# Odd-layer input projection: latents ahead of the last convolution slot, 512 and 320 columns wide, with ScalarE copies

## The chip, the cores and the metric

The kernel runs on one core of a Trainium2 chip. The metric is the device time of one execution in microseconds, the median of three runs. A profiled execution gives the trace; its rows are in microseconds from the start of its span.

## What is computed

Two layers of a diffusion backbone, batch 1, on 512 latent and 256 context tokens of width 1024, all in float32. The even layer is gMLP gating beside grouped-query attention; the odd layer, which is changed here, is a Conformer convolution beside multi-head latent attention. Each layer is followed by a gated ConvFFN. The odd mixer, cut to what matters:

```python
z = h_lat @ w_in                     # 1024 x (1024 conv, 512 zq, 256 zkv + 64 key rope)
c_lat = conformer_conv(z[..., :1024], conv_w, conv_b, ...)    # width 31, then channel norm, SiLU
q = mla_q(z[..., 1024:1536], g_cq, w_uq, cos, sin)            # rmsnorm, 512 -> 8 x (128 + 64), rope
k, v = mla_kv(z[..., 1536:], g_ckv, w_ukv, cos, sin)          # rmsnorm of 256, rope of 64, -> 8 x (128 + 128)
att = block_attention(q, [k_ctx, k], [v_ctx, v], scale)
o_lat = jnp.concatenate([c_lat, att], axis=-1) @ w_out
```

## The kernel before

Every weight matrix is cut into **slots** of 128 x 2048 floats (1 MB). SyncE loads slot n into one of two buffers (`w_load`); ScalarE rounds it (`round_hi`, L285) once slot n-2 is used; VectorE takes the rest (`take_lo`, L291); a product is then three matmuls, high x high, high x low, low x high. The semaphore `w_used` counts slots that TensorE has finished. VectorE and ScalarE carry out their instructions strictly in the order written, so the order in the code below is the plan.

The odd layer's projection is eight slots (`N_ODZ`). Slots 0 to 3 are convolution features: `feature_slot` puts 256 features with the weights stationary and 512 tokens moving, 48 matmuls of 512 columns. Between them VectorE forms G = a * sigmoid(b), and `conv_steps` spends single taps of the width-31 depthwise convolution (124 in all) wherever VectorE has room: `(0, 0, 8, 8, 12, 16, 12, 8)` in the slots, 16 in the query stage, 7 beside the keys and values, the other 37 two at a time beside the attention units. Slots 4 and 5 are the 512 features of zq, 256 each (`token_slot`, L335 to L337: tokens stationary, 256 columns moving, 4 token tiles); slots 6 and 7 are the 320 features of zkv with the key's rope part, 160 each, 6 token tiles. VectorE copies zq and zkv out of PSUM.

After slot 7 the **chains** run: ScalarE squares (L1476, L1482), VectorE the mean, GpSimd the power -1/2, VectorE the normalised value (L1979, L2032), TensorE transposes (L1668, L1681), VectorE `scaled` (gain, L2020), ScalarE rounds it (cqh, ckh), VectorE `low` (L2026). `UQ0` (L1692 to L1694, 4 token tiles, 48 matmuls) gives the rope part of the queries, copied by VectorE to QR, rotated (`rotate`), doubled by GpSimd to QRD. UQ0+1 and UQ0+2 give eight heads of queries into four PSUM banks, each copied by VectorE to QTn (L2064). `rope_transposes(0)` stands after head 5, `rope_transposes(4)` after head 7; the latter waits bank by bank for VectorE's `rope_lo` (L2070). Then follow keys and values (UKV0), and 32 attention units (8 heads x 4 query tiles).

The channel norm of the convolution (`CLN = 22`) is spread over the units: sum at unit 22, squares at 24 and 25, sum of squares at 28 (L1797), mean square and reciprocal at 29 (L2122, L2124), Sqrt on ScalarE at 30; the output projection `out_pe` waits for it, and for the modulation gate's row (L617, from `diag`).

## Time and profile before

| | |
|---|---|
| median of 3 runs | 1880.16 us (1879.54 to 1880.5) |
| profiled execution | 1880.5 us, span 1878.7 us |
| PE / DVE / ACT / POOL busy | 95% / 61% / 36% / 10% |
| mean granted TensorE clock | 0.977 of 2.4 GHz |
| odd layer's slots 2 to 7 | 1091.8 to 1168.9 us |
| from there to UQ0 | 15.0 us |
| attention units | about 1260 to 1406 us |

PE is TensorE's matmuls, PEld its weight loads, DVE VectorE, ACT ScalarE, POOL GpSimd. A displayed duration of a matmul is longer than its distance to the next one, because they are pipelined; what a stream costs is read from starts or from stretches. PEclk is the granted clock as a share of 2.4 GHz; 0.50 is 1.2 GHz.

### The profile page before, as it was taken

What the parts mean: (1) busy time and instruction counts of PE and PEld (TensorE: products, weight loads), DVE (VectorE), ACT (ScalarE), POOL (GpSimd) and SP (SyncE); (2) the same over time, 40 slices, a digit from 0 to 9 for tenths busy, and PEclk for the clock granted to TensorE, in tenths of its full rate; (3) what the DMA queues carried; (4) which work ended last, traced back from release to release, by engine and by line L of the source; (5) the groups of instructions that cost most, each with busy time, mean ns of one, the idle gap of its engine ahead of it and who ended that gap; (6) DMA issues with size and microseconds to landing.
All of it is one profiled execution on the core that took longest, in us unless ns stands there. A gap on an engine that the chain in (4) does not pass through costs nothing.

```text
span 1878.7 us, 24143 instructions
## 1 busy us (share of the span) xinstructions
PE 1779.5 (95%) x9514; PEld 1499.1 (80%) x9514; DVE 1140.5 (61%) x1714; ACT 671.4 (36%) x1095; POOL 179.4 (10%) x199
## 2 busy tenths in 40 slices
PE   6999799899999999999999999789988899999998
PEld 4777699777888888887777889569986788888776
DVE  4675567667666765644354778877855544344454
ACT  4342256534422122123343431144445432232342
POOL 1176400001200000000000200111210100000000
PEclk9999899999999999999999999899999899999999
DMA  8433000131234435522121121100002122322321
GB/s 352 155 112 113 23 1 2 57 101 46 101 117 153 146 137 189 193 72 84 45 90 47 56 103 68 45 23 1 2 10 103 68 90 91 110 89 89 112 91 67
DMA packets 30996, 166.80 MB, mean 89 GB/s; under 512 B 4144, under 2 KB 4656, under 8 KB 16688
## 3 DMA queue, kind: packets, MB, share of 16 engines
q1 hardware_dynamic: 29024, 163.60, 24.1%
q10 hardware_dynamic: 1872, 1.82, 0.3%
q8 instruction: 69, 1.13, 0.3%
q14 instruction: 31, 0.25, 0.0%
HBM read 163.31 MB, written 2.10 MB: 88 GB/s over the span
## 4 chain that ended last, share of the span: by engine, by line
PE 84%; DVE 6%; issue 4%; ACT 3%; POOL 1%; DVEq 1%; DMA 1%; POOLq 0%; ACTq 0%; SPq 0%
PE PS L302 12%; PE PS L304 12%; PE PS L306 12%; PE PS L603 8%; PE PS L605 7%; PE PS L604 7%; PE PS L1078 5%; PE PS L344 2%; PE PS L1066 2%; PE PS L345 2%; PE PS L346 2%; DVE w_lo L291 1%; PE PS L336 1%; PE PS L337 1%; PE PS L335 1%
## 5 line engine op out<-in xcount | busy, mean ns | idle before, releaser
L302 PE MATMUL PS<-HT,w_hi 128*128 128x512 f32 (+1 forms) x1232 | 377.7, 355 | 10.4 <-DVE HT L517 5.0
L304 PE MATMUL PS<-HT,w_hi 128*128 128x512 f32 (+1 forms) x1232 | 371.1, 350 | 0.0
L306 PE MATMUL PS<-HT,w_lo 128*128 128x512 f32 (+1 forms) x1232 | 370.1, 349 | 0.0
L291 DVE TENSOR_TENSOR w_lo<-w_raw,w_hi 128x2048 fp32r<-128x2048 f32 x103 | 237.1, 2303 | 157.8 <-ACT w_hi L285 153.6
L603 PE MATMUL PS<-w_hi,a_ring 128*128 128x512 f32 x680 | 277.1, 408 | 15.2 <-DVE a_ring L676 8.1
L604 PE MATMUL PS<-w_lo,a_ring 128*128 128x512 f32 x680 | 268.2, 394 | 0.0
L285 ACT ACTIVATE w_hi<-w_raw 128x2048 fp32r<-128x2048 f32 x103 | 196.3, 1906 | 157.5 <-PEq L635 69.4
L302 PEld LDWEIGHTS PS<-HT,w_hi 128*128 128x128 f32 x1232 | 206.4, 189 | 51.7 <-issue 6.5
L306 PEld LDWEIGHTS PS<-HT,w_lo 128*128 128x128 f32 x1232 | 207.2, 189 | 31.7
L304 PEld LDWEIGHTS PS<-HT,w_hi 128*128 128x128 f32 x1232 | 207.1, 189 | 30.4
L975 DVE SCALAR_TENSOR_TENSOR yb<-PS,cws,yb 128x511 f32<-128x511 f32 (+1 forms) x132 | 83.2, 658 | 169.2 <-ACTq L941 165.7
L603 PEld LDWEIGHTS PS<-w_hi,a_ring 128*128 128x128 f32 x680 | 129.7, 191 | 57.0 <-issue 27.3
L431 DVE SCALAR_TENSOR_TENSOR m_acc<-m_raw,sT,m_acc 128x1024 f32<-128x1024 f32 x112 | 145.6, 1331 | 27.8 <-DMA m_raw<-modu 22.9
L937 ACT ACTIVATE yb<-PS,cws 128x512 f32<-128x512 f32 x44 | 34.3, 780 | 347.2 <-PE PS L306 347.2
L604 PEld LDWEIGHTS PS<-w_lo,a_ring 128*128 128x128 f32 x680 | 129.8, 191 | 29.4 <-issue 3.4
L605 PE MATMUL PS<-w_hi,a_ring 128*128 128x512 f32 x340 | 135.4, 398 | 0.0
L826 POOL TENSOR_TENSOR rstd<-rstd,halfneg 128x1 f32<-128x1 f32 x20 | 12.6, 628 | 1223.2 <-DVE rstd L775 1223.2
L1964 DVE SCALAR_TENSOR_TENSOR cat_od<-G,ccw,cat_od 128x512 f32<-128x512 f32 x120 | 85.6, 756 | 3.0
L1131 DVE TENSOR_REDUCE rmax<-PS 128x1 f32<-128x768 f32 (+1 forms) x72 | 66.6, 925 | 32.1 <-PE PS L1041 23.2
L344 PE MATMUL PS<-w_hi,HT 128*128 128x512 f32 x192 | 77.3, 403 | 4.9 <-DVE HT L1847 4.0
L605 PEld LDWEIGHTS PS<-w_hi,a_ring 128*128 128x128 f32 x340 | 65.8, 194 | 14.5
L345 PE MATMUL PS<-w_lo,HT 128*128 128x512 f32 x192 | 76.0, 396 | 0.0
(309 smaller groups left out, 2811.9 us busy)
## 6 DMA issues: line engine op xcount, KB each, us to landing
w_raw<-wpack SPq DMA_DIRECT2D x103, 1024.0 KB, 4.8
m_raw<-modu SPq DMA_DIRECT2D x80, 512.0 KB, 4.2
mod_raw<-modw SPq DMA_DIRECT2D x8, 1024.0 KB, 12.2
X<-x SPq DMA_DIRECT2D x1, 2048.0 KB, 8.7
out<-X SPq DMA_DIRECT2D x4, 512.0 KB, 2.6
X<-ctx SPq DMA_DIRECT2D x1, 1024.0 KB, 10.9
alnb<-aln ACTq DMA_DIRECT2D x1, 512.0 KB, 4.3
csn<-rope_ev ACTq DMA_DIRECT2D x1, 256.0 KB, 2.6
```

The source lines that it names most:

```text
L285: nc.scalar.activation(w_hi[r][:, :], w_raw[r][:, :], ACT.Copy).then_inc(wh_ready, 1)
L291: nc.vector.tensor_tensor(w_lo[r][:, :], w_raw[r][:, :], w_hi[r][:, :].bitcast(F32), ALU.subtract).then_inc(wl_ready, 1)
L302: nc.tensor.matmul(o, wh, xh, start=start, stop=False)
L304: nc.tensor.matmul(o, wh, xl, start=False, stop=False)
L306: last = nc.tensor.matmul(o, wl, xh, start=False, stop=stop)
L344: nc.tensor.matmul(o, xh, w_hi[r][:, wc], start=k == 0, stop=False)
L345: nc.tensor.matmul(o, xh, w_lo[r][:, wc], start=False, stop=False)
L431: ops.scalar_tensor_tensor(out=acc[g][:, :], in0=raw[:, :], scalar=sT[:, k, g:g + 1], in1=acc[g][:, :], op0=ALU.mult, op1=ALU.add)
L603: nc.tensor.matmul(o, ah, w_hi[n % 2][:, wc], start=k == 0, stop=False)
L604: nc.tensor.matmul(o, ah, w_lo[n % 2][:, wc], start=False, stop=False)
L605: return nc.tensor.matmul(o, al, w_hi[n % 2][:, wc], start=False, stop=k == kt - 1)
L1078: last = nc.tensor.matmul(PS[:, 7, 0:w * P], V[:, k0 + j, c:c + P], PT[u % 2][:, j * w * P:(j + 1) * w * P], start=j == 0, stop=j == nk - 1)
```

## The change

The slots' order becomes conv 0, 1, 2, then zq (3, 4), zkv (5, 6), then conv 3 as slot 7. A latent slot now holds half of the 1024 input features (four k-tiles) for all its columns: zq with 512 columns, zkv with 320 (`wide` with a bank and a width), accumulating over two slots in PSUM. ScalarE squares and copies each finished tile; the zq chain goes to slots 5 and 6, the zkv chain to slot 7, the zq transposes into slot 6, those of zkv into UQ0. ScalarE also copies QR and the eight heads. The taps are spread anew (47 in the slots, 28 in the query stage); the channel norm is two units later, and its Sqrt is in the output projection. At the start of the kernel, `mod_products` waits for both halves of a chunk at once. QR moves to the start of region R_A. Most deleted lines are left out of the diff; they are in the listing above.

```diff
-        QR = at("QR", R_MOD, [P, LT, 512])
+        QR = at("QR", R_A, [P, LT, 512])
...
-        mod_landed = [sem(f"mod_landed{i}") for i in range(KD)]
+        mod_landed = [sem(f"mod_landed{i}") for i in range(4)]
...
+        def wide(n, t, k, bank=None, w=512):
+            r, o, wc = n % 2, PS[:, t if bank is None else bank, 0:w], slice(k % 4 * w, k % 4 * w + w)
...
+            pe.wait_ge(mod_landed[c], 32)
             for i in range(2):
-                pe.wait_ge(mod_landed[2 * c + i], 16)
...
-        CLN = 22
+        CLN = 24
+        CONV_SLOTS, CONV_BANKS = (0, 1, 2, 7), (0, 3, 0, 6)
+        ZQ_BANKS, ZKV_BANKS, CQ_BANKS = (3, 4, 2, 5), (6, 7, 0, 1, 3, 4), (2, 5)
...
+            def cq_hi(k):
+                act.wait_ge(S("odn", "aff"), k + 1)
+                dst = cqh[:, k, :] if k < 4 else ckh[:, k - 4, :]
+                nc.scalar.activation(dst, ev_t[k % 2][:, 0:LAT if k < 4 else TOK], ACT.Copy).then_inc(S("odn", "hi"), 1)
             for s in range(N_ODZ):
                 if s:
                     round_hi(act, OD0 + s + 1)
-                if s < 4:
+                if s in CONV_SLOTS:
...
                     act.wait_ge(w_used, OD0 + s + 1)
...
+                if s == 4:
+                    for t in range(LT):
+                        act.wait_ge(S("odz", "acc"), t + 1)
+                        nc.scalar.activation(zjunk[:, :], PS[:, ZQ_BANKS[t], :], ACT.Square, accum_out=ssq[:, t:t + 1])
+                        act.drain()
+                        nc.scalar.activation(zq[:, t, :], PS[:, ZQ_BANKS[t], :], ACT.Copy).then_inc(S("odz", "copy"), 1)
+                    act.drain().then_inc(S("odq", "ssq"), 1)
                 if s == 6:
...
+                    for t in range(NT):
+                        act.wait_ge(S("odz", "acc"), LT + t + 1)
+                        nc.scalar.activation(zjunk[:, 0:256], PS[:, ZKV_BANKS[t], 0:256], ACT.Square,
+                                             accum_out=ssq[:, 16 + t:17 + t])
+                        act.drain()
+                        nc.scalar.activation(zkv[:, t, :], PS[:, ZKV_BANKS[t], 0:320], ACT.Copy)\
+                            .then_inc(S("odz", "copy"), 1)
+                        if t < 4:
+                            cq_hi(t)
+                    act.drain().then_inc(S("odkv", "ssq"), 1)
+            round_hi(act, UQ0 + 1)
+            def rope_out(t):
+                act.wait_ge(S("odu", "rmm"), t + 1)
+                nc.scalar.activation(QR[:, t, :], PS[:, t, :], ACT.Copy).then_inc(S("odu", "qr"), 1)
+            rope_out(0)
+            rope_out(1)
+            cq_hi(4)
+            rope_out(2)
+            rope_out(3)
+            cq_hi(5)
+            def query_out(h):
+                act.wait_ge(S("odu", "qmm"), h + 1)
+                nc.scalar.activation(QTn[:, h, :], PS[:, h % 4, :], ACT.Copy).then_inc(S("odu", "q"), 1)
+            query_out(0)
             round_hi(act, UQ0 + 2)
+            for h in range(1, 6):
+                query_out(h)
             act.wait_ge(S("odn", "krt"), 1)
             for p in range(HEADS):
                 h = (p + 4) % HEADS
                 if p == 4:
+                    query_out(6)
+                    query_out(7)
...
-                if u == CLN + 8:
-                    act.wait_ge(S("cln", "var"), 1)
+            attn_act(act, "od", True, units(True), 192 ** -0.5, beside_units)
+            def beside_out(q):
+                if q == 2:
+                    act.wait_ge(S("cln", "var"), 2)
...
+            def zq_transposes(k):
+                pe.wait_ge(S("odq", "xn"), 1)
+                if k >= 2:
+                    pe.wait_ge(S("odn", "aff"), k - 1)
+                for t in range(LT):
+                    last = nc.tensor.transpose(PS[:, CQ_BANKS[k % 2], t * P:(t + 1) * P], zq[:, t, k * P:(k + 1) * P],
+                                               ident[:, :])
+                last.then_inc(S("odn", "tr"), 1)
             for s in range(N_ODZ):
                 n = OD0 + s
...
-                if s >= 2:
-                    pe.wait_ge(S("odz", "evac"), s - 1)
...
-                elif s < 4:
...
+                elif s in CONV_SLOTS:
+                    if s == 2:
+                        pe.wait_ge(S("odz", "evac"), 1)
+                    else:
+                        pe.wait_ge(S("odz", "copy"), LT + 2)
+                    last = feature_slot(s, n, LAT, bank=CONV_BANKS[CONV_SLOTS.index(s)])
+                elif s < 5:
+                    if s == 3:
+                        pe.wait_ge(S("odz", "evac"), 2)
+                    for t in range(LT):
+                        for k in range(4 * (s - 3), 4 * (s - 3) + 4):
+                            last = wide(n, t, k, ZQ_BANKS[t])
+                        if s == 4:
+                            last.then_inc(S("odz", "acc"), 1)
                 else:
-                    if s == 6:
+                    if s == 5:
...
+                        pe.wait_ge(S("odz", "evac"), 3)
+                    for t in range(NT):
+                        if s == 5 and t >= 4:
+                            pe.wait_ge(S("odz", "copy"), t - 3)
+                        for k in range(4 * (s - 5), 4 * (s - 5) + 4):
+                            last = wide(n, t, k, ZKV_BANKS[t], 320)
+                        if s == 6:
+                            last.then_inc(S("odz", "acc"), 1)
+                            if t < 4:
+                                zq_transposes(t)
+                if s in (4, 6):
+                    pe.drain().then_inc(w_used, 1)
+                else:
+                    last.then_inc(w_used, 1)
             def key_transposes(k):
                 if k == 4:
-                    pe.wait_ge(S("odn", "aff"), 2)
+                    pe.wait_ge(S("odkv", "xn"), 1)
+                    pe.wait_ge(S("odn", "aff"), 4)
                 elif k == 5:
-                    pe.wait_ge(S("odn", "aff"), 4)
+                    pe.wait_ge(S("odz", "evac"), 4)
                 else:
                     pe.wait_ge(S("odn", "aff"), 5)
                 for t in range(NT):
                     src = zkv[:, t, (k - 4) * P:(k - 3) * P] if k < 6 else kr2[:, t, :]
                     last = nc.tensor.transpose(ps2(4 + 2 * (k % 2), TOK)[:, t * P:(t + 1) * P], src, ident[:, :])
                 last.then_inc(S("odn", "tr"), 1)
...
+            pe.wait_ge(S("odz", "copy"), LT + NT)
             pe.wait_ge(S("odn", "lo"), 4)
             n = UQ0
...
                 last.then_inc(S("odu", "rmm"), 1)
+                if t in (1, 3):
+                    key_transposes(4 + t // 2)
...
+            TAPS = (0, 0, 10, 12, 13, 9, 3, 0, 24)
...
-                conv_steps((0, 0, 8, 8, 12, 16, 12, 8)[s], range(min(s, 4)))
-                if s == 7:
+                conv_steps(TAPS[s], range(min(s, 3)))
+                if s == 5:
                     dve.wait_ge(S("odq", "ssq"), 1)
...
                         .then_inc(S("odq", "mean"), 1)
...
                     for t in range(LT):
                         last = nc.vector.tensor_scalar(zq[:, t, :], zq[:, t, :], rstd[:, t:t + 1], None, ALU.mult)
                     last.then_inc(S("odq", "xn"), 1)
-                b = 3 * (s % 2)
-                dve.wait_ge(w_used, OD0 + s + 1)
+                if s == 6:
+                    scaled(0)
+                    scaled(1)
+                    low(0)
+                    scaled(2)
+                    low(1)
+                    scaled(3)
+                    low(2)
+                    low(3)
+                if s == 7:
...
+                    dve.wait_ge(S("odkv", "ssq"), 1)
...
+                        .then_inc(S("odkv", "mean"), 1)
+                    for t in range(LT):
...
+                    dve.wait_ge(S("odkv", "rstd"), 1)
+                    for t in range(NT):
+                        last = nc.vector.tensor_scalar(zkv[:, t, 0:256], zkv[:, t, 0:256], rstd[:, 16 + t:17 + t], None,
+                                                       ALU.mult)
+                    last.then_inc(S("odkv", "xn"), 1)
...
+            take_lo(dve, UQ0 + 1)
+            scaled(4)
+            conv_steps(2)
+            low(4)
+            scaled(5)
+            conv_steps(2)
+            low(5)
...
+                dve.wait_ge(S("odu", "qr"), t + 1)
...
+                rotate(dve, zz[:, :, :, 0], zz[:, :, :, 1], csd[:, 0, t, :].unsqueeze(1).to_broadcast([P, 8, 32]),
...
+                dve.drain().then_inc(S("odu", "rope"), 1)
+                if t == 1:
                     dve.wait_ge(S("odn", "tr"), 7)
                     nc.vector.tensor_copy(KRT[:, :], ps2(4, TOK)).then_inc(S("odn", "krt"), 1)
...
+                if t == 2:
+                    take_lo(dve, UQ0 + 2)
+            conv_steps(TAPS[8])
...
-                    nc.vector.tensor_scalar(mu[:, :], PS[:, 6, :], 1.0 / 512, EPS, ALU.mult, ALU.add)
+                    nc.vector.tensor_scalar(mu[:, :], PS[:, 6, :], 1.0 / 512, EPS, ALU.mult, ALU.add)\
+                        .then_inc(S("cln", "var"), 1)
...
+    conv = _slots_in(od, [np.concatenate([r(P * j, P * j + P), r(512 + P * j, 512 + P * j + P)]) for j in range(4)])
+    zq = [_k_cols(od[512 * h:512 * h + 512], r(1024, 1536)) for h in range(2)]
+    zkv = [_k_cols(od[512 * h:512 * h + 512], r(1536, 1856)) for h in range(2)]
+    slots += conv[:3] + zq + zkv + conv[3:]
```

## Rows read from the trace of the kernel before

**Rows 1.** Page: the span, then busy time and share of each engine
```profile
span 1878.7 us, 24143 instructions
...
PE 1779.5 (95%) x9514; PEld 1499.1 (80%) x9514; DVE 1140.5 (61%) x1714; ACT 671.4 (36%) x1095; POOL 179.4 (10%) x199
```

**Rows 2.** Busy time by stretch: length, PE, PEld, DVE, ACT, POOL, PEclk, DMA share, GB/s
```profile
1102.90:1113.70 10.80, 10.80 (x50) 8.93 (x49) 8.44 (x10) 2.40 (x2) 0.00 (x0) 1.00 0.29 97
1113.70:1136.70 23.00, 23.00 (x193) 23.00 (x192) 20.49 (x26) 4.32 (x3) 0.00 (x0) 1.00 0.27 93
1136.70:1168.90 32.20, 32.20 (x290) 32.13 (x288) 27.41 (x40) 6.51 (x10) 1.02 (x1) 1.00 0.19 66
1168.90:1183.90 15.00, 6.67 (x29) 5.56 (x28) 13.14 (x45) 6.85 (x17) 1.33 (x1) 0.66 0.00 1
1183.90:1196.90 13.00, 12.72 (x48) 10.08 (x49) 9.97 (x12) 1.88 (x4) 0.00 (x0) 0.87 0.23 81
1196.90:1234.20 37.30, 29.23 (x134) 23.33 (x134) 31.26 (x53) 9.94 (x11) 4.17 (x4) 0.91 0.08 29
```

**Rows 3.** Timeline of TensorE before UQ0: start us, us, instruction, [idle before, releaser]
```profile
1170.37 3.52 PE L1668 MATMUL PS<-ident,zq 128*128 128x128 f32 x16 [1.38 <-DVE zkv L1998]
...
1183.94 0.79 PE L1692 MATMUL PS<-w_hi,cqh 128*128 128x512 f32 x1 [0.71 <-DVE cql L2026]
...
1184.96 0.63 PE L1694 MATMUL PS<-w_hi,cql 128*128 128x512 f32 x1
1185.39 0.63 PE L1692 MATMUL PS<-w_hi,cqh 128*128 128x512 f32 x1
```

**Rows 4.** Timeline of TensorE, query stage
```profile
1213.61 0.80 PE L302 MATMUL PS<-cqh,w_hi 128*128 128x512 f32 x1 [4.83 <-DVE w_lo L291]
...
1221.23 1.91 PE L1706 MATMUL PS<-ident,QRD 128*128 128x128 f32 x16
...
1230.19 2.39 PE L1706 MATMUL PS<-ident,QRD 128*128 128x128 f32 x16 [1.60 <-DVE QS L2070]
1234.29 0.59 PE L302 MATMUL PS<-ckh,w_hi 128*128 128x512 f32 x2 [1.71 <-issue]
```

**Rows 5.** Timeline of ScalarE, first square of zq
```profile
1143.21 0.63 ACT L1476 ACTIVATE sg<-zq 128x512 f32<-128x512 f32 x1 [4.32 <-DVE zq L1993]
```

**Rows 6.** Timeline of VectorE, projection and query stage
```profile
1130.63 11.34 DVE L1964 SCALAR_TENSOR_TENSOR cat_od<-G,ccw,cat_od 128x512 f32<-128x512 f32 x16
...
1164.08 1.67 DVE L1979 TENSOR_SCALAR zq<-zq,rstd 128x512 f32<-128x512 f32 x4 [1.13 <-POOL rstd L484]
...
1199.96 0.69 DVE L2064 COPY QTn<-PS 128x512 f32<-128x512 f32 x1 [0.22 <-PE PS L306]
...
1203.21 0.69 DVE L2064 COPY QTn<-PS 128x512 f32<-128x512 f32 x1 [0.17 <-issue]
...
1229.35 2.52 DVE L2070 TENSOR_TENSOR QS<-PS,QS 64x512 fp32r<-64x512 f32 x4
1231.90 4.49 DVE L291 TENSOR_TENSOR w_lo<-w_raw,w_hi 128x2048 fp32r<-128x2048 f32 x2
```

**Rows 7.** Timelines of VectorE, TensorE and ScalarE, end of the attention
```profile
1397.16 3.35 DVE L2124 RECIPROCAL rs_b<-mu 128x512 f32<-128x512 f32 x1
...
1401.29 0.87 PE L1066 MATMUL PS<-ident,Pod 128*128 128x128 f32 x6 [1.79 <-DVE Pod L1142]
1403.07 2.93 PE L1078 MATMUL PS<-PTo,Vod 128*128 128x128 f32 x12 [0.90 <-ACT PTo L1117]
...
1416.16 2.08 PE L617 MATMUL PS<-diag,ones 128*128 128x512 f32 x2 [3.15 <-DVE diag L769]
...
1411.08 1.91 ACT L285 ACTIVATE w_hi<-w_raw 128x2048 fp32r<-128x2048 f32 x1 [8.07 <-DMA w_raw<-wpack]
```

**Rows 8.** Line 388 (mod_products): durations min/median/max, starts; then idle by releaser
```profile
L388 PE MATMUL PS<-mod_raw,s x64: 592/592/617, 20.7 to 55.5; 128*32 128x512 f32 x64
...
  issue: 3.3, 11
```

More of the change, by code:

```diff
@@ L323, in feature_slot @@
             return last
-        def token_slot(ns, n, tiles, width, between=lambda step: None):
-            b, r = 3 * (ns % 2), n % 2
-            last = None
-            for t in range(tiles):
-                o = PS[:, b + t // 2, (t % 2) * 256:(t % 2) * 256 + width]
-                for k in range(KD):
-                    between(t * KD + k)
-                    wc = slice(k * 256, k * 256 + width)
-                    xh, xl = (HT[:, t // 2, w, k, t % 2 * P:t % 2 * P + P] for w in range(2))
-                    nc.tensor.matmul(o, xh, w_hi[r][:, wc], start=k == 0, stop=False)
-                    nc.tensor.matmul(o, xh, w_lo[r][:, wc], start=False, stop=False)
-                    last = nc.tensor.matmul(o, xl, w_hi[r][:, wc], start=False, stop=k == KD - 1)
-            return last
-        def wide(n, t, k):
-            r, o, wc = n % 2, PS[:, t, :], slice(k % 4 * 512, k % 4 * 512 + 512)
+        def wide(n, t, k, bank=None, w=512):
+            r, o, wc = n % 2, PS[:, t if bank is None else bank, 0:w], slice(k % 4 * w, k % 4 * w + w)
             xh, xl = (HT[:, t // 2, w, k, t % 2 * P:t % 2 * P + P] for w in range(2))
@@ L2002, in _ @@
-            const_ready(dve, "csd", 1)
-            dve.drain()
-            for t in range(LT):
-                kr = zkv[:, t, 256:320].rearrange("p (i two) -> p i two", two=2)
-                rotate(dve, kr[:, :, 0], kr[:, :, 1], csd[:, 0, t, :], csd[:, 1, t, :], rA[:, 0:32], rB[:, 0:32])
-            for half in range(2):
-                nc.vector.tensor_copy(kr2[:, :, 64 * half:64 * half + 64], zkv[:, :, 256:320])
-            dve.wait_ge(S("odkv", "ssq"), 1)
-            nc.vector.tensor_scalar(rstd[:, 16:16 + NT], ssq[:, 16:16 + NT], 1.0 / 256, EPS, ALU.mult, ALU.add)\
-                .then_inc(S("odkv", "mean"), 1)
@@ L2176, in _k_cols @@
     kt = w.shape[0] // P
-    return w[:, cols].reshape(kt, P, len(cols)).transpose(1, 0, 2).reshape(P, SLOT)
+    out = np.zeros((P, SLOT), w.dtype)
+    out[:, :kt * len(cols)] = w[:, cols].reshape(kt, P, len(cols)).transpose(1, 0, 2).reshape(P, kt * len(cols))
+    return out
 def _rope(d_rot):
```

143 lines of the change are left out of this document (41 added, 102 removed).

## The prediction

> **What bounds the kernel now.** I read the page's busy shares first: TensorE is busy 95% of a span of 1878.7 us [rows 1], so time can come only from cheaper TensorE work or from the few gaps. The odd layer's input projection was then cut into stretches [rows 2]. In the first three of them PE is busy to the last tenth at a granted clock of 1.00: one convolution slot of 48 matmuls, 512 wide, takes 10.8 us (0.225 each); the two zq slots, 192 matmuls 256 wide, take 23.0 us (0.120 each); the two zkv slots, 288 matmuls 160 wide, take 32.2 us (0.112 each). Each token tile takes 8 k-tiles x 3 products per slot (4 tiles for zq, 6 for zkv; the (x) of a stretch counts a matmul that lies across its edge too). The reader should see that 160 columns cost almost as much as 256: the narrow ones pay for something other than columns, and the weight load beside them is busy 32.13 of 32.20 us.
>
> The fourth stretch is a gap: 15.0 us with 28 transposes in it. PE waits there for the copy of zkv, later for the scaled and low parts, and starts the query projection only at 1183.94 [rows 3], because the chain square, mean, power, normalise, transpose, scale, round, low runs with nothing beside it. The clock falls to its lower level (1.2 of 2.4 GHz: mean 0.66 in the gap) and is still 0.87 in the next stretch. The query stretch (1196.9 to 1234.2) is 37.3 us for about 29 us of PE work; it waits 4.83 us for VectorE's low part of slot UQ0+2, 1.60 for the rope's low parts, and 1.71 before the first key, which the row calls issue but which ends with the low part of UKV0 [rows 4, 6].
>
> **Part by part.** (a) zkv wide. 144 matmuls of 320 columns replace 288 of 160. No row has 320 columns; the nearest are 256 (0.120) and 512 (0.225), so the bounds are 17.3 and 32.4 us. On the line between them 320 lies at 0.147: 21.2 us, a gain of 11.0. I take this, since 256 is much nearer. The trace's 0.112 at 160 columns is what makes the gain. The Trainium skill, "TensorE: Matmul & The Clock Gate", section "Back-to-back issue gap", gives N/2.4 + 2.5 ns for an isolated pair, 69 ns at 160 columns and 136 at 320, by which the two forms would cost the same 19.8 us and this part would give nothing; the row of 112 ns contradicts it for this stream.
>
> (b) zq wide: 192 x 0.120 = 23.0 becomes 96 x 0.225 = 21.6, a gain of 1.4.
>
> (c) The gap. Its 15.0 us go. Put back: the 28 transposes, now inside slot 6 and UQ0, at 1.91/16 = 0.12 each [rows 4], 3.4 us; two TensorE drains after slots 4 and 6, at the 0.5 that UQ0's stretch leaves (13.0 less 48 x 0.225 and less the slow start of (d)), 1.0; and a new wait. In slot 6 the first zq transposes follow tile 0, and need zq normalised. After slot 4: ScalarE finishes the last square (0.63) and a copy of the same 512 columns (taken as 0.63, with 0.3 for the sum's read-out), then rounds slot 6's weights (1.9); VectorE takes the low part (2.2), 9 taps at 11.34/16 = 0.70 (6.3), the mean (0.2), waits for the power (1.1), normalises (1.7) [rows 5, 6, 7]. That is 14.8 and a wake-up or two, say 15.1. PE has slot 5 (10.6), tile 0 of slot 6 (1.8) and a drain (0.5): 12.9. So it waits about 2.2, and I charge 1.7 for a clock dip behind it: after the 1.38 us before the first transposes the clock fell [rows 2, 3], and eight matmuls at the lower level cost 1.7 below. Sum of (c): -15.0 + 3.4 + 1.0 + 2.2 + 1.7 = -6.7. Bounds of the wait and dip: 0 and 8.
>
> (d) UQ0 took 13.0 us; it starts at full clock when conv slot 7 runs straight before it. Gain 1.7: at 1183.94 PE began slow, one matmul every 0.43 [rows 3], and the 13.0 us hold room for about eight such, 8 x 0.2. Everything the wait ahead of UQ0 needs should be ready: the zq low parts end in slot 6, the last zkv copies soon after it, and slot 7's 10.8 us cover the zkv mean, the key's rope, and the normalising. UQ0's own cover is its weights, rounded a slot earlier.
>
> (e) Query stage. VectorE loses twelve copies (QR and QTn) of 0.69 [rows 6] to ScalarE, which is idle there, but gets 28 taps (2 + 2 + 24) where it had 16, and its rotations no longer alternate with heads. From UQ0's end its chain is: scale and low of k = 5 (1.0 each), 2 taps 1.4, four rotations at 3.25 (one head copy's start to the next) - 0.6 = 2.6 (10.4), KRT copy 1.0, low part of UQ0+2 2.2, 24 taps 16.9, four rope lows 2.5, low of UKV0 2.2: 38.6 until the first key. Before it was 37.3 from the same point. With the wake-ups I take +1.5. PE would finish its share (two slots of 10.8, 38 transposes 4.6, drains 1.0) in about 27 and so idles some 9 us: about 2 before UQ0+2's weights, about 7 before the last rope transposes. Bounds: -3 (VectorE gets ahead) and +9 (ScalarE's in-order queue, where `cq_hi(5)` stands before `query_out(0)` and the weight rounding before `query_out(1)`, holds banks or the rotations). The later scores hang on the same POOL chain as before: 0.
>
> (f) Attention. Taps left beside the units go from 37 to 42; they lie in units paced by PE, price 0, with 5 x 0.70 = 3.5 if no cover. The channel norm moves two units later. Its reciprocal takes 3.35 us on VectorE and stood before the normalising of the last unit: PE waited 1.79 for Pod and ran the last twelve value products in 2.93, slow [rows 7]. Now mean-square and reciprocal follow the last unit, and the Sqrt goes into the output projection. Gain 1.8 plus at most 1.4 of clock: I take 3.0, bounds 0 and 4. What replaces it: PE waits for `var` to reach 1, a copy and one 0.7 us read, then runs 24 products; but it stands 3.15 us at line 617 anyway, behind the DMA that starts at attention's end (ScalarE waits 8.07 for it) and VectorE's diag [rows 7]. If that cover is gone it costs 1.1. The Sqrt and its table load delay ScalarE's third part by some 1.9, under the same wait.
>
> (g) `mod_products` waits for both halves. Of its 64 matmuls none sat behind a DMA; the only idle before them is issue [rows 8]: the second half had landed. 0. The memory placements of QR and zjunk, the weight slots (eight still, 1 MB each) and SP's queue order: same count, same triggers, 0.
>
> **Sum:** -11.0 - 1.4 - 6.7 - 1.7 + 1.5 - 3.0 = -22.3. The profiled execution took 1880.5 us (1.8 beyond its span), 0.34 above the median of 1880.16; so 1858.2 for it, 1857.9 for the median.
>
> **Rivals.** *The query stage gives back more.* For it: it is already VectorE-bound, and 24 taps in one block stand before the rope lows that PE waits for. Against: the copies leave. At the bound of (e), 7.5 more: 1865. *No wait in slot 6.* If slot 5's taps end early, 3.9 more gained: 1854. *Width pays nothing:* at the upper bound of (a) 320 columns cost as 512 (0.225 each, 32.4 us), and (a) turns to zero: 1869. The section of the Trainium skill named in (a) would have it zero too. Against it: 256 columns cost 0.120. *The wait re-forms before UQ0:* PE needs the zq lows and all zkv copies there, and slot 7 as well as slot 5 wait for banks; if ScalarE, with 16 instructions per slot pair more, lags by a slot, the gain of (c), (d) and (f) is gone and most of (a) is waited away: about 1879. Against: ScalarE is busy 6.5 of 32.2 us now.
>
> *Slower: the clock.* PE now pauses briefly at many places (tile waits in slots 5 and 6, drains, UQ0+2, the rope) instead of once. If these hold the lower level from slot 6 through UQ0+1, 47 us of stream cost 0.43 instead of 0.225 per matmul, 41 us more: 1899. It decides once the lower level lasts longer than 25 us of stream. Against it: before, the clock came back within UQ0's stretch (0.87) and in the query stretch, with three waits, it was 0.91. The Trainium skill describes just this, PE pausing between groups as it cycles through PSUM banks and its clock going up and down, in "TensorE: Matmul & The Clock Gate", section "A second HAM failure mode: psum-queue depth-cycling"; the trace shows single dips of this kind, no lasting one.
>
> **How the numbers follow.** Forecast 0.68, more given back 0.12, no wait 0.10, width nothing 0.04, wait re-forms 0.03, clock 0.03. The range takes in the forecast with the bounds of (c), (e) and (f) and the first two rivals: 1850 to 1866.5. A change within 0.2% (3.8 us) can't be told from none: that is the re-formed wait alone. Faster 0.94, same 0.03, slower 0.03.
>
> **What would show it.** Slots 5 and 6 at 10.6 us each plus transposes; conv slot 7 followed by UQ0 with no gap; one PE wait near 2 us on zq and one near 7 on QS; UQ0 at clock 1.00; no wait for Pod in the last unit. Wrong would be: 320-wide spacing away from 0.147, low clock through slot 7, or a first key more than 42 us after UQ0's end.

## The result and the profile after

The changed kernel takes 1858.36 us (median; 1858.18 to 1858.55), the kernel before 1880.09 in the same rounds: ratio 0.9885, 95% interval 0.9867 to 0.9902. The forecast was 1857.9. The profiled execution has a span of 1856.6 us against 1878.7, 22.1 less. The page of the changed kernel answers to [rows 1]:

```profile
span 1856.6 us, 23682 instructions
...
PE 1757.4 (95%) x9274; PEld 1474.3 (79%) x9274; DVE 1131.2 (61%) x1692; ACT 682.6 (37%) x1117; POOL 179.6 (10%) x199
```

Its stretches answer to [rows 2], with the same columns. They are: zq (slots 3 and 4), zkv's first half (5), its second half with the zq transposes (6), the last convolution slot (7), UQ0 with twelve key transposes, and the query stage up to the first key.

```profile
1102.10:1124.00 21.90, 21.90 (x98) 17.93 (x96) 19.15 (x24) 8.19 (x12) 0.00 (x0) 1.00 0.27 96
1124.50:1135.10 10.60, 10.58 (x72) 10.60 (x73) 9.97 (x14) 2.90 (x4) 0.00 (x0) 1.00 0.29 100
1135.10:1151.00 15.90, 12.92 (x90) 12.14 (x88) 12.77 (x20) 8.28 (x21) 1.02 (x1) 1.00 0.19 66
1151.00:1162.00 11.00, 10.91 (x48) 9.09 (x49) 7.37 (x34) 2.69 (x4) 1.41 (x1) 1.00 0.27 97
1162.00:1174.70 12.70, 12.47 (x62) 10.19 (x60) 6.48 (x9) 5.64 (x7) 0.00 (x0) 1.00 0.24 83
1174.70:1216.50 41.80, 29.81 (x134) 24.50 (x134) 39.59 (x60) 15.15 (x20) 4.17 (x4) 0.85 0.07 26
```

The reader should see two things. Up to UQ0 only slot 6 has waits for data, and the clock is 1.00 throughout; the 15.0 us gap is gone. Behind UQ0 the query stage is longer than before, 41.8 us against 37.3, with VectorE busy for 39.59 of it. TensorE's timeline shows its waits (start, duration, line, idle before and releaser):

```profile
1139.37 0.66 PE L1658 MATMUL PS<-ident,zq 128*128 128x128 f32 x4 [2.30 <-DVE zq L2028]
...
1144.50 0.63 PE L1658 MATMUL PS<-ident,zq 128*128 128x128 f32 x4 [0.51 <-DVE ev_t L2009]
...
1190.42 0.80 PE L303 MATMUL PS<-cqh,w_hi 128*128 128x512 f32 x1 [3.86 <-DVE w_lo L292]
...
1212.47 3.65 PE L1738 MATMUL PS<-ident,QRD 128*128 128x128 f32 x16 [7.72 <-DVE QS L2089]
1216.58 0.91 PE L303 MATMUL PS<-ckh,w_hi 128*128 128x512 f32 x2 [0.46 <-issue]
```

VectorE's timeline, query stage, shows what it did meanwhile: UQ0+2's low part in 3.16 us where 2.2 was counted, a rotation's first product in 1.29, and 24 taps in 18.87.

```profile
1180.61 1.29 DVE L1170 TENSOR_TENSOR rA<-QR,csd 128x256 f32<-128x256 f32 x1 [0.17 <-issue]
...
1187.21 3.16 DVE L292 TENSOR_TENSOR w_lo<-w_raw,w_hi 128x2048 fp32r<-128x2048 f32 x1 [0.17 <-issue]
...
1192.75 18.87 DVE L1997 SCALAR_TENSOR_TENSOR cat_od<-G,ccw,cat_od 128x512 f32<-128x512 f32 x24 [0.21 <-issue]
```

At the end of the attention, which answers to [rows 7], there is no wait for Pod and the last twelve products take 1.60 us instead of 2.93. The output projection's products begin behind the read of the variance, and the stall behind diag is still there:

```profile
1382.64 1.60 PE L1064 MATMUL PS<-PTo,Vod 128*128 128x128 f32 x12 [0.90 <-ACT PTo L1103]
1385.23 0.50 PE L589 MATMUL PS<-w_hi,a_ring 128*128 128x512 f32 x1 [0.98 <-DVE mu L2141]
1394.50 1.83 PE L603 MATMUL PS<-diag,ones 128*128 128x512 f32 x2 [3.53 <-DVE diag L755]
```

So the time went as follows, by the starts of the same instructions: slot 2's first matmul 1091.78 to 1091.18 (0.6 earlier, ahead of the change's main part); UQ0's end 22.2 earlier (1196.9 to 1174.7); the first key 17.7 earlier (4.5 given back); the first diag product of the output projection 21.7 earlier (1416.16 to 1394.50, 4.0 gained); the end 22.1.

### The profile page after: what moved, and what is told of

Same layout as the page of the kernel before. It is cut to its first block, busy times and chain, and to the rows that moved or that the text cites. A ratio compares the mean times of both kernels' runs of the same rounds, so it can differ in the third digit from the quotient of the medians.

```text
span 1856.6 us, 23682 instructions
## 1 busy us (share of the span) xinstructions
PE 1757.4 (95%) x9274; PEld 1474.3 (79%) x9274; DVE 1131.2 (61%) x1692; ACT 682.6 (37%) x1117; POOL 179.6 (10%) x199
## 3 DMA queue, kind: packets, MB, share of 16 engines
q10 hardware_dynamic: 1872, 1.82, 0.3%
## 4 chain that ended last, share of the span: by engine, by line
PE 83%; DVE 7%; issue 4%; ACT 3%; POOL 1%; DVEq 1%; DMA 1%; ACTq 0%; POOLq 0%; SPq 0%
PE PS L303 12%; PE PS L307 12%; PE PS L305 12%; PE PS L589 8%; PE PS L590 7%; PE PS L591 7%; PE PS L1064 5%; PE PS L330 3%; PE PS L332 3%; PE PS L331 3%; PE PS L1052 2%; DVE w_lo L292 2%; ACT w_hi L286 1%; DVE pre_tmp_pre L497 1%; PE PS L1030 1%
## 5 line engine op out<-in xcount | busy, mean ns | idle before, releaser
L589 PEld LDWEIGHTS PS<-w_hi,a_ring 128*128 128x128 f32 x680 | 129.5, 190 | 58.3 <-issue 27.4
L330 PE MATMUL PS<-w_hi,HT 128*128 128x512 f32 (+1 forms) x272 | 105.0, 386 | 5.0 <-DVE HT L1879 3.9
L331 PE MATMUL PS<-w_lo,HT 128*128 128x512 f32 (+1 forms) x272 | 103.1, 379 | 0.0
L332 PE MATMUL PS<-w_hi,HT 128*128 128x512 f32 (+1 forms) x272 | 103.1, 379 | 0.0
```

Source lines behind the costliest of these rows:

```text
L330: nc.tensor.matmul(o, xh, w_hi[r][:, wc], start=k == 0, stop=False)
L331: nc.tensor.matmul(o, xh, w_lo[r][:, wc], start=False, stop=False)
L332: return nc.tensor.matmul(o, xl, w_hi[r][:, wc], start=False, stop=k == KD - 1)
L589: nc.tensor.matmul(o, ah, w_hi[n % 2][:, wc], start=k == 0, stop=False)
```

## The experiments

All are edits of the changed kernel. Each row gives the median, the ratio to the kernel before with its interval, and two lengths from the profile: from slot 2's first matmul (S) to the first key product, and from S to the first diag product of the output projection (O). The last row says why the lengths are needed. The lengths vary by themselves too, at two places that are shown below the table: up to 0.9 us in slot 6, and up to 2.6 us behind the first wait for Pod.

| kernel | median us | ratio, 95% interval | S to key | S to O |
|---|---|---|---|---|
| before | | | 142.51 | 324.38 |
| changed | 1858.36 | 0.9885 (0.9867-0.9902) | 125.40 | 303.32 |
| zkv in halves | 1866.45 | 0.9926 (0.9912-0.9939) | 133.03 | 310.86 |
| zq in halves | 1855.47 | 0.9870 (0.9855-0.9885) | 127.49 | 305.39 |
| 3 taps, slot 5 to 7 | 1855.63 | 0.9879 (0.9861-0.9898) | 123.48 | 302.42 |
| zq chain behind slot 7 | 1865.96 | 0.9921 (0.9908-0.9935) | 130.40 | 309.28 |
| norm 2 units earlier | 1860.46 | 0.9898 (0.9882-0.9913) | 125.41 | 307.32 |
| the same, and Sqrt | 1858.57 | 0.9890 (0.9874-0.9907) | 126.27 | 307.87 |
| 12 taps beside units | 1850.53 | 0.9851 (0.9833-0.9869) | 119.86 | 299.70 |
| QRD copies on ScalarE | 1854.60 | 0.9867 (0.9852-0.9882) | 122.88 | 302.09 |
| low part earlier | 1855.60 | 0.9874 (0.9859-0.9889) | 125.40 | 303.13 |
| together | 1842.85 | 0.9804 (0.9789-0.9820) | 109.84 | 291.68 |
| together, GpSimd copies | 1846.03 | 0.9831 (0.9817-0.9844) | 111.50 | 291.80 |
| changed, once more | 1857.41 | 0.9891 (0.9874-0.9907) | 126.28 | 302.66 |

**The changed kernel once more.** No edit.

> The changed kernel itself once more, in rounds like those of the experiments. In their profiles slot 2 of the odd projection, far ahead of everything edited, starts at 1087.0 to 1091.4 us, and the part behind the attention takes 455.6 or 457.7 us. Theory (these two places vary from one execution to the next, with TensorE's clock near the program's start and late in the last feed-forward, whatever the kernel): this kernel too gives times between 1854 and 1860, median 1856 to 1858, and from slot 2's start to the output projection's first wait 303.3 us, within 1.2. Rival (the experiments' edits moved the early part): all runs within 0.3 us of 1858.4, as the four before.

The times were 1851.49, 1856.8, 1858.02 and 1859.56. The length S to O is 302.66, within the 1.2 named; S itself starts at 1084.65, earlier than the range given, and one time lies below 1854. The rival falls: the spread is there with no edit at all. One place is seen in the windows of 30 to 35 us, first the changed kernel's first profile, then this one:

```profile
30.00:35.00 5.00, 4.62 (x11) 3.68 (x12) 1.70 (x3) 0.03 (x1) 0.00 (x0) 0.50 1.02 424
```

```profile
30.00:35.00 5.00, 4.98 (x26) 4.27 (x27) 1.34 (x2) 0.00 (x0) 0.00 (x0) 1.00 1.01 418
```

Eleven matmuls against 26 in the same 5 us. The experiments' medians therefore move by a few us for a reason outside the edits, and a difference of 3 us between two of them is read from the lengths.

The lengths have their own spread. Key comes 0.9 later here than in the first profile, all of it lost in slot 6 (last section), and from key to O it is 176.38 against 177.92. The latter lies in the 10 us behind the attention's first wait for Pod, which is 3.80 us in every profile. The windows are of the changed kernel's first profile, of this one, and of the experiment with three taps moved:

```profile
1244.20:1254.20 10.00, 10.00 (x58) 9.01 (x59) 4.93 (x10) 5.44 (x10) 0.92 (x2) 0.83 0.01 2
```

```profile
1238.60:1248.60 10.00, 10.00 (x67) 9.08 (x68) 6.26 (x13) 6.35 (x12) 0.92 (x2) 1.00 0.01 2
```

```profile
1238.50:1248.50 10.00, 10.00 (x49) 9.00 (x50) 4.29 (x9) 5.26 (x10) 0.72 (x2) 0.72 0.01 2
```

From that wait to O it is 150.3 us at 0.83, 148.7 at 1.00 and 151.3 at 0.72. The kernel before stands at 0.83, like the first profile. So 1.0 us of a key-to-O length is the clock's where the window shows about 0.7, and it is taken off below.

**zkv in halves.**

```diff
-            nc.tensor.matmul(o, xh, w_hi[r][:, wc], start=k == 0, stop=False)
...
+            for a in (0, h) if bank is not None and w in (320,) else (None,):
+                a, e = (0, w) if a is None else (a, a + h)
+                o, wc = PS[:, t if bank is None else bank, a:e], slice(k % 4 * w + a, k % 4 * w + e)
+                nc.tensor.matmul(o, xh, w_hi[r][:, wc], start=k == 0 and a == 0, stop=False)
...
```

> The changed kernel with each zkv product of 320 columns issued as two of 160 (288 matmuls again, same slots, order, banks and chains). Theory (width pays, as forecast): 288 x 0.112 = 32.3 us in place of 144 x 0.1465 = 21.1, 11.2 us more of stream; slot 5 and tile 0 of slot 6 become some 6.5 us longer, which covers the 2.3 us wait for the normalised zq and the 0.5 at the third group, so the time rises by 8.4 to 8.9 us: 1867. Rival (time goes by columns, width pays nothing): 160 columns take half of 320, 0.073 each, no change: 1858. Rival (what was gained came from the order, not from the width): rise under 3 us.

Key and O come 7.6 and 7.5 us later, the median 8.1. The window over slot 5 of this kernel:

```profile
1123.90:1139.90 16.00, 16.00 (x144) 16.00 (x144) 13.02 (x20) 2.85 (x4) 1.02 (x1) 1.00 0.18 67
```

That is 0.111 per matmul of 160 columns with the weight load busy all the time, against 10.58/72 = 0.147 for 320. For all 288: 32.0 us against 21.1. The wait for zq fell to nothing, as foreseen. Time by columns alone is refuted: half the columns cost three quarters of the time.

**zq in halves.** The same edit for the 512 columns of zq.

> The changed kernel with each zq product of 512 columns issued as two of 256. Theory: 192 x 0.120 = 23.0 us in place of 96 x 0.227 = 21.8, all of it ahead of slot 5 on TensorE, nothing to absorb it: +1.2 us, 1859.6. Rival (the wait in slot 6 is set by VectorE's taps, not by the end of slot 4, and absorbs it): 0, 1858.4. Rival (a change of stationary operand per 256 columns costs more in this order than before): over +3.

Slot 5 starts 34.59 after S instead of 33.34: 1.25, the theory's 1.2. The key comes 2.1 later; the other 0.9 is not the edit's: it is lost in slot 6, and the unedited kernel loses 0.9 at the same place in its second profile (below). The median shows neither, being 2.9 below the first median of the changed kernel: too small a term for that measure.

**Three taps from slot 5 to slot 7.**

```diff
-            TAPS = (0, 0, 10, 12, 13, 9, 3, 0, 24)
+            TAPS = (0, 0, 10, 12, 13, 6, 3, 3, 24)
```

> The changed kernel with three convolution taps moved from slot 5 to slot 7, nothing else. VectorE normalises zq 3 x 0.70 = 2.1 us earlier, scales the first zq group 2.1 earlier too. Theory: the 2.30 us wait before the first zq transposes shrinks to about 0.2 and the 0.51 one at the third group with it, the clock was at its full level through both, so the time falls by 2.1 to 2.6 us: 1856. Rival (a dip hidden in the spacing after the wait, as the forecast charged): by about 4, 1854.5. Rival (VectorE's chain in the query stage sets the end, and it has the three taps either way): the wait goes but reappears as a longer wait for QS or for the low part of UQ0+2, 0 to -0.5.

The 2.30 wait is gone, the one at the third group grew to 0.80; UQ0 and the key come 1.9 earlier, O only 0.9 earlier. So 2.3 less the 0.3 that moved was gained, and no hidden dip was there. The 1.0 that O lacks is lost behind the wait for Pod, where the clock is 0.72 instead of 0.83; the unedited kernel's two profiles differ there by more, so it is not shown to be the edit's.

**The zq chain behind slot 7.** The sixteen zq transposes, the scales, roundings and low parts stand after the last convolution slot. Only TensorE's part is shown; ScalarE's `cq_hi` and VectorE's `scaled` and `low` move likewise.

```diff
-                            if t < 4:
-                                zq_transposes(t)
...
+            for k in range(4):
+                zq_transposes(k)
             pe.wait_ge(S("odz", "copy"), LT + NT)
```

> The changed kernel with the zq transposes, scales, roundings and low parts behind the last convolution slot, in front of UQ0, instead of inside slot 6 and beside slot 7; squares, mean and normalising stay where they are. Theory (a chain costs when nothing is beside it): eight VectorE steps of 0.7 with ScalarE's 0.6 between, less the transposes that run meanwhile, leave TensorE idle for 6 to 7 us before UQ0; the 2.8 us of waits inside slot 6 are gone; a pause of that length brings the clock's lower level into UQ0, 1.7 us: +5 to +6 in all, 1864. Rival (the query stage is bound by VectorE, whose work is the same): VectorE had idle time beside slots 6 and 7 that it now fills with nothing, so the same or up to +9. Rival (the chains were hidden anyway or cost only their transposes): within 1 us of 1858.

```profile
1159.91 1.29 PE L1658 MATMUL PS<-ident,zq 128*128 128x128 f32 x8 [1.55 <-DVE ev_t L2009]
1164.88 0.76 PE L1722 MATMUL PS<-w_hi,cqh 128*128 128x512 f32 x1 [3.69 <-issue]
1165.45 0.63 PE L1723 MATMUL PS<-w_lo,cqh 128*128 128x512 f32 x1
```

TensorE idles 1.55 + 3.69 = 5.2, a little under the 6 to 7 named, UQ0 begins at the lower clock with one matmul every 0.43 us and takes 15.1 instead of 12.7, and the key comes 5.0 later, O 6.0 (of which 0.9 is the clock behind Pod). UQ0 starts 2.6 later: the new idle time less the 2.8 us of waits that left slot 6. The gain of the chain's place is thus 2.6 us of waiting and 2.4 us of clock. VectorE's bound behind UQ0 did not absorb it. The zkv chain, the other part of the old gap, was not moved back.

**The channel norm two units earlier**, then the same with the square root at unit 30.

```diff
-        CLN = 24
+        CLN = 22
...
-                conv_steps(min(2, 31 * 4 - sum(taps)))
+                conv_steps(min(3 if u < 4 else 2, 31 * 4 - sum(taps)))
```

> The changed kernel with the channel norm two units earlier again (sum at unit 22, mean square and reciprocal beside unit 29; three taps each in the first four units so that the convolution ends in time), the square root left in the output projection. Theory (the 3.35 us reciprocal on VectorE in front of the last unit's normalising is what cost): TensorE waits about 1.8 us for Pod again and runs the last value products slower: +3.0 to +3.9, 1861.5 to 1862.3. Rival (the square root and its table load on ScalarE, among the exponentials, cost): 0 here. Rival (three taps in a unit hold up the first units): + up to 2.8 more, seen as waits at units 0 to 3.

> As the run before it, and the square root at unit 30 again, as in the kernel before. Theory (the reciprocal is the cause): the same as without it, within 0.5 us, 1861.5 to 1862.3. Rival (the square root with its table load on ScalarE is the cause or part of it): another 1 to 3.9 us on top.

```profile
1381.03 0.88 PE L1052 MATMUL PS<-ident,Pod 128*128 128x128 f32 x6 [1.81 <-DVE Pod L1128]
1382.80 2.93 PE L1064 MATMUL PS<-PTo,Vod 128*128 128x128 f32 x12 [0.90 <-ACT PTo L1103]
```

This is [rows 7] again, behind a reciprocal that runs from 1376.90 for 3.35. Key unchanged, O 4.0 later: 1.81 of wait, 1.33 of slower products, and a 0.71 wait for the last low part of the keys, in front of the norm's sum in an earlier unit. The clock behind the first wait for Pod is 0.83 in both, so this 4.0 is free of it. With the square root also moved, key to O is 181.60 against 181.91 without it, and the last waits are the same (1.82 for Pod), though its table load and wait stand on ScalarE between the last unit's exponentials and its copy of PTo. The reciprocal is the cause; the square root, which runs while TensorE waits behind the reciprocal, adds nothing.

**Twelve taps beside the units.**

```diff
-            TAPS = (0, 0, 10, 12, 13, 9, 3, 0, 24)
+            TAPS = (0, 0, 10, 12, 13, 9, 3, 0, 12)
...
-                conv_steps(min(2, 31 * 4 - sum(taps)))
+                conv_steps(min(3 if u < 12 else 2, 31 * 4 - sum(taps)))
```

> The changed kernel with 12 of the 24 taps that stand before the rope's low parts moved beside the attention's first twelve units (three a unit instead of two). Theory (VectorE's chain bounds the query stage): the 7.72 us wait for QS shrinks by 12 x 0.75 = 9.0 to nothing, the time falls by about 7.5: 1851. Rival (what bounds the query stage is ScalarE's order, or the rope copies on GpSimd): the wait stays, 0. Rival (VectorE has no room beside the units): 9.0 us come back as waits in units 0 to 11, 1859.

```profile
1202.37 1.94 PE L1738 MATMUL PS<-ident,QRD 128*128 128x128 f32 x16 [0.37 <-issue]
1206.86 0.59 PE L303 MATMUL PS<-ckh,w_hi 128*128 128x512 f32 x2 [2.56 <-issue]
```

```profile
1204.47 4.49 DVE L292 TENSOR_TENSOR w_lo<-w_raw,w_hi 128x2048 fp32r<-128x2048 f32 x2 [2.94 <-ACT w_hi L286]
```

The wait for QS went from 7.72 to 0.37, and the key came 5.5 earlier, not 7.5: a wait of 2.56 stands before it, where 0.46 stood. VectorE has already been waiting 2.94 there for the rounding of UKV0's weights, which ScalarE holds behind two query copies. From key to O it then took 1.9 more, 1.0 of it the clock behind Pod (0.72 here), so that the twelve taps cost about 0.9 beside the units. The theory is right in kind and its size was 3.9 too large by O: 2.0 for what was late next, 1.9 behind the key. That the median fell by 7.8, near the 7.5 named, is luck: O gained 3.6, the rest lies in the variation outside the edit.

**QRD copies on ScalarE.**

```diff
-                nc.gpsimd.tensor_copy(QRD[:, t, :, :].rearrange("p h (d c) -> p h d c", d=2),
...
+                for d in range(2):
+                    last = nc.scalar.activation(QRD[:, t, :, 64 * d:64 * d + 64],
+                                                QR[:, t, :].rearrange("p (h c) -> p h c", c=64), ACT.Copy)
...
+                if h < 5:
+                    rope_dup(h - 1)
```

> The changed kernel with the four copies of the rotated queries into QRD on ScalarE (two of 128 x 512 each) behind query_out(1) to (4), instead of on GpSimd. Theory (VectorE is slowed while GpSimd copies: 3.16 us for the low part of UQ0+2 where 2.2 was forecast, 1.29 for a rotation's product, taps of 1.5): the low part returns to 2.2 to 2.5 us, the rotation's product to 0.42, the tap block is 1 to 2 us shorter; first key 2 to 3 us earlier, 1855.5 to 1856.5. Rival (the operations are slow for another reason, or the shape of the tap block itself is): VectorE's durations stay, 0. Rival (ScalarE's order then holds up the query copies): + up to 3.

```profile
1180.29 0.42 DVE L1170 TENSOR_TENSOR rA<-QR,csd 128x256 f32<-128x256 f32 x1 [0.17 <-issue]
...
1186.03 2.29 DVE L292 TENSOR_TENSOR w_lo<-w_raw,w_hi 128x2048 fp32r<-128x2048 f32 x1 [0.17 <-issue]
...
1190.70 18.11 DVE L2000 SCALAR_TENSOR_TENSOR cat_od<-G,ccw,cat_od 128x512 f32<-128x512 f32 x24 [0.21 <-issue]
```

Three VectorE stretches lose 0.87, 0.87 and 0.76 us, and the key comes 2.5 earlier, just their sum. In the changed kernel each of the three began within 0.1 us of a GpSimd copy of 1.04 us:

```profile
1180.58 1.04 POOL L1317 COPY QRD<-QR 128x1024 f32<-128x1024 f32 x1 [22.68 <-DVEq L2077]
...
1187.18 1.04 POOL L1317 COPY QRD<-QR 128x1024 f32<-128x1024 f32 x1 [2.25 <-DVEq L2077]
1192.68 1.04 POOL L1317 COPY QRD<-QR 128x1024 f32<-128x1024 f32 x1 [4.46 <-DVEq L2077]
```

The Trainium skill, "SBUF — State Buffer", section "Who interferes with whom", says that a VectorE instruction with both inputs in SBUF contends with a GpSimd one that reads SBUF, and that whichever issues first holds the port for its whole length while the other is blocked. The runs agree: in all three GpSimd began first, by 0.03 to 0.07 us, and the delay is nearly a copy's length, however long the VectorE instruction is. The fourth copy stood beside the KRT copy out of PSUM, which was not slowed (0.96 in both kernels).

The kernel before has the same four copies, and there they cost almost nothing, because a query copy out of PSUM stood beside each:

```profile
1199.88 1.04 POOL L1329 COPY QRD<-QR 128x1024 f32<-128x1024 f32 x1 [23.38 <-DVEq L2060]
...
1210.38 1.04 POOL L1329 COPY QRD<-QR 128x1024 f32<-128x1024 f32 x1 [2.25 <-DVEq L2060]
```

```profile
1200.57 0.63 DVE L1184 TENSOR_TENSOR rA<-QR,csd 128x256 f32<-128x256 f32 x1
...
1211.01 2.55 DVE L291 TENSOR_TENSOR w_lo<-w_raw,w_hi 128x2048 fp32r<-128x2048 f32 x1
```

Three VectorE instructions began in the rest of a copy and lost 0.2 to 0.3 each (0.63 for 0.42, 2.55 for 2.29), 0.7 in all. Moving the query copies to ScalarE thus took away what had hidden the contention. O came only 1.2 earlier, of the 2.5; 1.0 of the rest is the clock behind Pod (0.69 here).

**UQ0+2's low part after the first rotation.**

```diff
-                if t == 2:
+                if t == 0:
                     take_lo(dve, UQ0 + 2)
```

> The changed kernel with the low part of UQ0+2's weights taken after the first rotation instead of after the third, nothing else. Theory (VectorE's chain from the end of UQ0 to the low part of UKV0 sets the first key, and the wait for UQ0+2 is only where part of the slack shows): TensorE's 3.86 us wait goes, and the 7.72 us wait for QS grows by 3.9 to about 11.6; the first key comes at the same time within 0.5 us, 1858. Rival (each wait is a cost of its own): 3.9 us faster, 1854.5.

```profile
1182.68 0.47 PE L303 MATMUL PS<-cqh,w_hi 128*128 128x512 f32 x1 [0.26 <-issue]
1189.61 1.97 PE L1738 MATMUL PS<-ident,QRD 128*128 128x128 f32 x16 [1.23 <-POOL QRD L1317]
1208.32 3.65 PE L1738 MATMUL PS<-ident,QRD 128*128 128x128 f32 x16 [11.27 <-DVE QS L2089]
```

The 3.86 wait is gone and reappears: 11.27 instead of 7.72, and the key stands 125.40 after S in both. Of the two waits neither had a price of its own; the chain on VectorE had.

**Together**, with the QRD copies on ScalarE and then on GpSimd.

```diff
+                    round_hi(act, UKV0)
                     query_out(6)
                     query_out(7)
-                    round_hi(act, UKV0)
...
-            TAPS = (0, 0, 10, 12, 13, 9, 3, 0, 24)
+            TAPS = (0, 0, 10, 12, 13, 6, 3, 3, 6)
...
             take_lo(dve, UQ0 + 1)
+            conv_steps(2)
             scaled(4)
             conv_steps(2)
             low(4)
+            conv_steps(4)
             scaled(5)
...
-                if t == 2:
+                if t == 0:
                     take_lo(dve, UQ0 + 2)
...
-                conv_steps(min(2, 31 * 4 - sum(taps)))
+                conv_steps(min(3 if u < 12 else 2, 31 * 4 - sum(taps)))
```

> The pieces together, on the changed kernel: three taps from slot 5 to slot 7; of the 24 taps before the rope's low parts, six stay, six go into VectorE's two idle times of 1.4 and 3.0 us before its scales of the key latents, twelve beside the attention's first twelve units; UQ0+2's low part after the first rotation; UKV0's weights rounded before the last two query copies; the QRD copies on ScalarE. Theory: the waits of 2.30 (zq), 3.86 (UQ0+2), 7.72 (QS) and 0.46 (first key) all go, 14.3 us; attention gives back about 1 for twelve taps, and the rope's own latency leaves 1 to 2: first key 12 us earlier counted from slot 2's start, time 1845 to 1847. Rival (the waits only change places): the single experiments' -2, -5.5 and -2.5 overlap and no more than -7 is left, 1851.

> The same, with the QRD copies left on GpSimd. Theory (once VectorE has slack in the query stage its slowing by GpSimd's copies costs nothing): the same first key within 0.5 us, 1845 to 1847; UQ0+2's low part and a rotation's product are slow again (3.1 and 1.3 us) and nobody waits for them. Rival (VectorE still bounds it): 2.5 us later than with the copies on ScalarE. Rival (ScalarE was what was short): up to 2 earlier.

```profile
1182.03 0.47 PE L303 MATMUL PS<-cqh,w_hi 128*128 128x512 f32 x1 [0.26 <-issue]
1188.54 1.97 PE L1741 MATMUL PS<-ident,QRD 128*128 128x128 f32 x16 [0.78 <-ACT QRD L1497]
1196.35 1.94 PE L1741 MATMUL PS<-ident,QRD 128*128 128x128 f32 x16 [0.36 <-issue]
1198.04 0.60 PE L303 MATMUL PS<-ckh,w_hi 128*128 128x512 f32 x2
...
1204.34 0.62 PE L303 MATMUL PS<-ckh,w_hi 128*128 128x512 f32 x2 [1.81 <-DVE KNl L2104]
```

The key comes 15.6 us earlier, O 11.6, and the median is 1842.85, below both kernels: the interval lies wholly under the changed kernel's. Of the 15.6 the keys' stage and the units gave back 3.9. With the copies on GpSimd the key is 1.7 later, behind a 2.48 us wait for QRD instead of 0.78, so the theory's 0.5 was wrong there; O is the same within 0.1. The clock explains both. Behind the 1.81 wait, which both kernels have, it fell in the first (upper window) and not in the second:

```profile
1206.00:1208.00 2.00, 2.00 (x8) 1.71 (x7) 0.65 (x1) 0.64 (x1) 0.00 (x0) 0.50 0.00 0
```

```profile
1207.50:1209.50 2.00, 2.00 (x13) 1.77 (x12) 1.08 (x2) 0.81 (x1) 0.00 (x0) 1.00 0.00 0
```

From the first product behind that wait to the first score it is 11.80 against 10.23, 1.6 us; that ate the lead of the ScalarE copies. With the 1.0 behind Pod (0.73 in both), 2.6 of the 3.9 given back is clock. Whether the fall goes with the edit or with the execution is open, with one profile of each. From O on the two profiles are equal; the medians differ by 3.2, about what the start's clock alone can make.

## Why the prediction was right

The time was right to 0.5 us, and partly by luck: misses cancelled. By the lengths of the first pair of profiles, slot 2 to the end of UQ0 gained 21.6 where (a) to (d) said 20.8; the query stage gave back 4.5 where (e) said 1.5; key to O gained 4.0 where (f) said 3.0; and 0.6 ahead of slot 2 and 0.4 behind O were in no term. Together they make the 22.1 of the span.

- **(a) and (b), width:** forecast 12.4, measured 11.0 and 1.1 by the windows. The halved kernels show it directly: 10.9 and 1.25. The straight line between 256 and 512 columns was right at 320 (it gives 0.146; 0.147 was measured). The formula of the Trainium skill, "TensorE: Matmul & The Clock Gate", "Back-to-back issue gap", would give 136 ns at 320 and 69 at 160, hardly any gain (19.6 us against 19.9). The Trainium skill gives it there for isolated matmuls and itself calls it too low at small widths. The stream's 147 and 111 ns agree with that warning. Not all of the gain arrives: 3 of the 10.9 us lay over the wait in slot 6.
- **(c) and (d), the gap:** zq, zkv and the gap took 70.2 us; the same work now takes 59.9 - 11.0 = 48.9, 21.3 less. Of the 28 transposes twelve now stand in UQ0; without their 1.4, (a) to (c) said 20.5. The wait was forecast at 2.2 and is 2.30, with 0.51 before the third group that no term had. The dip of 1.7 behind it was charged and isn't there in the first profile; in three of the others it is, and costs 0.9. UQ0 takes 12.7 with its twelve transposes; 13.0 - 1.7 + 1.4 says 12.7.
- **(e), the query stage:** the term that was mis-sized. +1.5 forecast, +4.5 measured, inside its bounds; the miss is 3.0, where the rival named 7.5. The mechanism was the named one, a VectorE chain with PE waiting for UQ0+2's weights (about 2 said, 3.86) and for QS (about 7 said, 7.72). The chain's own sum, 38.6 against about 27 of TensorE's work, leaves over 11 of idle time, not the 9 that were said; 12.0 was measured. The miss has two parts. GpSimd's copies hold up VectorE by 2.5, of which the sum had about 0.7 unseen in the rotations it took from [rows 6]: 1.8. And a tap was taken at 0.70 from one block [rows 6], where 24 take 18.11 with nothing beside them, 0.75 each: 1.2. Each tap takes 0.75 by itself in both kernels. Two in a row that overlap, in the kernel before, and two that do not, in the changed one:

```profile
1130.63 1.41 DVE L1964 SCALAR_TENSOR_TENSOR cat_od<-G,ccw,cat_od 128x512 f32<-128x512 f32 x2
```

```profile
1195.16 1.58 DVE L1997 SCALAR_TENSOR_TENSOR cat_od<-G,ccw,cat_od 128x512 f32<-128x512 f32 x2
```

The next tap starts 0.67 later when it is for another group of channels, and 0.83 later behind the drain that `conv_steps` puts in where the same group comes again. In [rows 6] a drain stands before every fourth. The changed order brings the fourth group of convolution features last, so its taps come in a row: ten gaps of 0.82 to 0.83 at the head of the block of 24. No run rearranges them. The wait of 3.9 for the weights has no part in the miss, since it can be moved at no change.
- **(f), the attention's end:** 3.0 forecast, 4.0 measured and 4.0 by undoing it. The 1.1 for the variance was rightly covered by the stall behind diag. The 0.7 wait for the keys' low part is the term that was missed.
- **(g):** nothing was seen; slot 2 starts 0.6 earlier in the first pair of profiles, which is within what the start varies by itself. Those two have the lower clock at 30 to 35 us alike (0.51 and 0.50), so their difference is free of it. All 38 executions of the kernel before lie between 1876.1 and 1881.1, the eight of the changed kernel between 1851.5 and 1859.6; whether the edit at the start has to do with the wider spread is open.

Small slips in the forecast's sums change nothing: the terms of the wait in (c) add up to 15.0, not 14.8, and 47 us of stream at the lower clock would cost 43 more, not 41.

The rivals: the lasting low clock and the wait re-formed before UQ0 did not occur (clock 1.00 from slot 3 to UQ0's end in the first profile). Beside those, the forecast's marks hold: slot 5 at 10.6, slot 7 followed by UQ0 with no gap, no wait for Pod. The first key came 41.9 us after UQ0's end, at the edge of the 42 that was to be wrong.

Undone one at a time, the 320 columns, the 512 columns, the zq chain's place and the norm's place cost 7.6, 1.2, 5.0 and 4.0 at O or the key, 17.8 of the 22.1. These need not add up, since the wait in slot 6 hides part of the first. The place of the zkv chain, the order of the slots and the copies on ScalarE were not undone by themselves.

## What to carry to other kernels

When a chain is moved to a place where the matrix engine is busy, write out the whole queue of the engine that runs it, up to the next wait of the matrix engine: here a gap of 15.0 us went, and 4.5 came back one stage later as a longer VectorE chain. A wait shows where slack ends, not what costs: moving one instruction erased a wait of 3.9 us and changed nothing, while thinning the chain before the last wait paid, until the next engine in line (ScalarE's rounding) was late. Before moving a copy out of PSUM off VectorE, see which GpSimd copy it stands beside: here it had kept 1.8 us of contention hidden. Compare small edits by lengths between the same instructions, not by whole times, when the start of the program varies by more than the edit, and look at the clock inside the lengths too.
